# Half of the Strassen weight sums of the down projections: from VectorE to accumulating transfers

## What is computed

```python
def swiglu(h, w_gate, w_up, w_down):
    return (jax.nn.silu(h @ w_gate) * (h @ w_up)) @ w_down   # h: 256 x 2048, w_down: 5632 x 2048

h = rmsnorm(x, norm_ffn_pre[l])
x = x + rmsnorm(swiglu(h, w_ffn_gate[l], w_ffn_up[l], w_ffn_down[l]), norm_ffn_post[l])
```

## Time and profile before

| | |
|---|---|
| time, median of 3 runs | 2452.81 us (2452.26 to 2452.99) |
| time of the profiled execution | 2453.34 us |
| its span in the trace | 2451.5 us |
| TensorE busy | 2408.9 us (98%) |
| VectorE busy | 1799.5 us (73%) |
| ScalarE busy | 1223.0 us (50%) |
| GpSimd busy | 99.2 us (4%) |
| read from HBM | 503.06 MB |

### The profile page before, as it was taken

How to read it: one execution, slowest core, us unless ns; L and a number is a source line. 1 busy time by engine, 2 the same in 40 slices (tenths; PEclk the granted TensorE clock), 3 DMA queues, 4 the chain that set the end, 5 groups by cost and what they waited for, 6 DMA issues and landing times.

```text
span 2451.5 us, 28699 instructions
## 1 busy us (share of the span) xinstructions
PE 2408.9 (98%) x11138; PEld 1998.8 (82%) x11138; DVE 1799.5 (73%) x2366; ACT 1223.0 (50%) x1587; POOL 99.2 (4%) x150
## 2 busy tenths in 40 slices
PE   5999999999999999999999999999999999999998
PEld 4888888888788888888888888888888888888887
DVE  6998988766776675767777678965776766758776
ACT  4757665445544444444444544544544444445443
POOL 1210000000000000000000212000000000000000
PEclk8999999999999999999999999999999999999999
DMA  9997655564565566555656655445555565565654
GB/s 383 357 384 248 244 190 171 183 251 150 175 198 194 189 193 199 191 189 182 231 187 208 197 189 193 168 148 196 182 196 189 192 198 194 189 195 182 223 189 155
DMA packets 189495, 507.06 MB, mean 207 GB/s; under 512 B 17792, under 2 KB 18080, under 8 KB 188080
## 3 DMA queue, kind: packets, MB, share of 16 engines
q1 hardware_dynamic: 177008, 456.92, 55.3%
q0 software_dynamic: 11824, 46.14, 5.1%
q10 hardware_dynamic: 528, 2.16, 0.2%
HBM read 503.06 MB, written 2.10 MB: 206 GB/s over the span
## 4 chain that ended last, share of the span: by engine, by line
PE 95%; DVE 3%; DMA 1%; ACT 0%; issue 0%; SPq 0%; DVEq 0%; ACTq 0%
PE acc L677 29%; PE acc L679 29%; PE acc L678 29%; PE wk L1119 1%; PE wk L1118 1%; PE wk L1120 1%; DVE gate L1798 1%; PE wk L703 1%; DMA raw<-in_ada_w 1%; DMA raw<-in_w_in 1%; PE acc L1119 1%; PE acc L1118 1%; PE acc L1120 1%; DVE lo L1823 0%; PE wk L1190 0%
## 5 line engine op out<-in xcount | busy, mean ns | idle before, releaser
L677 PE MATMUL acc<-hi,h 128*128 128x512 f32 x2592 | 1017.3, 392 | 2.1 <-ACT proj L1384 0.7
L679 PE MATMUL acc<-hi,h 128*128 128x512 f32 x2592 | 1009.6, 389 | 0.0
L678 PE MATMUL acc<-lo,h 128*128 128x512 f32 x2592 | 1009.0, 389 | 0.0
L1823 DVE SCALAR_TENSOR_TENSOR lo<-raw,gcols,hi 128x1024 fp32r<-128x1024 f32 (+1 forms) x464 | 569.1, 1270 | 184.1 <-ACT hi L1269 181.5
L1269 ACT ACTIVATE hi<-raw,gcols 128x1024 fp32r<-128x1024 f32 (+1 forms) x464 | 497.4, 1128 | 380.7 <-PE acc L679 315.5
L1821 DVE TENSOR_TENSOR lo<-raw,hi 128x1024 fp32r<-128x1024 f32 (+2 forms) x428 | 486.7, 1187 | 121.8 <-ACT hi L1269 120.2
L677 PEld LDWEIGHTS acc<-hi,h 128*128 128x128 f32 x2592 | 486.9, 188 | 104.6 <-issue 3.7
L679 PEld LDWEIGHTS acc<-hi,h 128*128 128x128 f32 x2592 | 486.6, 188 | 102.2
L678 PEld LDWEIGHTS acc<-lo,h 128*128 128x128 f32 x2592 | 486.9, 188 | 99.1
L1269 ACT ACTIVATE hi<-raw 128x1024 fp32r<-128x1024 f32 (+2 forms) x428 | 413.5, 1026 | 275.1 <-DMA raw<-in_w_ffn_down 114.8
L677 PE MATMUL acc<-hi,g_hi 128*128 128x512 f32 x544 | 211.9, 390 | 0.0
(11 more groups left out here) (369 smaller groups left out, 1589.6 us busy)
## 6 DMA issues: line engine op xcount, KB each, us to landing
raw<-in_w_ffn_gate SPq DMA_DIRECT2D x176, 512.0 KB, 3.8
raw<-in_w_ffn_up SPq DMA_DIRECT2D x176, 512.0 KB, 4.6
raw<-in_w_ffn_down SPq DMA_DIRECT2D x176, 512.0 KB, 5.0
raw<-in_w_in SPq DMA_DIRECT2D x144, 512.0 KB, 4.8
raw<-in_w_kv SPq DMA_DIRECT2D x64, 512.0 KB, 4.8
ada_raw<-in_ada_w POOLq DMA_DIRECT2D x38, 512.0 KB, 7.7
gate_raw<-in_ada_w POOLq DMA_DIRECT2D x32, 512.0 KB, 6.3
raw<-in_w_out SPq DMA_DIRECT2D x32, 512.0 KB, 5.1
```

The lines of the kernel that those rows point to most:

```text
L677: pe.matmul(o, l_hi, w_hi[:, c], start=first, stop=False, skip_group_check=loaded)
L678: pe.matmul(o, l_hi, w_lo[:, c], start=False, stop=False, skip_group_check=loaded)
L679: mm = pe.matmul(o, l_lo, w_hi[:, c], start=False, stop=last, skip_group_check=loaded)
L1823: ins = vec.scalar_tensor_tensor(out=lo[:, r, c], in0=raw[:, r, c], scalar=gcols[:, st.gain, k:k + 1], in1=hi[:, m % HI_SLOTS, c], op0=ALU ...
```

## The change

Two of the four sums are no longer made by VectorE. b12 + b22 is made by a transfer that reads b22 from HBM and adds it to b12 where that lies in SBUF. t1 is made in two steps: SyncE loads b11 from HBM into the place of t1, and a second accumulating transfer adds b12 to it. VectorE still makes t2 and t4.

- SyncE has one more transfer of 256 KB for every slab of sums, on the semaphore `sum_loaded`, issued when the place in the ring is free.
- GpSimd issues two accumulating transfers of 256 KB for each Strassen slab (`sums_by_transfer`), the first when the slab has landed, the second when b11 has landed too. Both count on `sums_landed`. It runs for group 0 ahead of the load of `gain_a` and for group 1 behind it.
- ScalarE waits for both transfers ahead of the high part of a Strassen slab; before, it waited for lines 1858 and 1859. VectorE waits for both ahead of t2.
- Some semaphores are merged (`post0_in` and `post1_in`, `r_d_last` and `r_d_mid`, `k2_rotated` and `q2_rotated`), with waits at the same points of the same engines.

```diff
@@ sync, for each slab m
             if is_sums(m):
+                sp.wait_ge(slab_used, m - RING + 1)
+                src, (a, b), how = slabs[m - 1][0].src(slabs[m - 1][1], slabs[m - 1][2], 0)
+                sp.dma_start(raw[:, place(m) % RING, 0:HALF], src[:, 0:HALF]).then_inc(sum_loaded, 16)
                 continue
@@ scalar, conv
             if is_sums(m):
-                act.wait_ge(sums_made, 2 * sum(is_sums(i) for i in range(m + 1)))
+                act.wait_ge(sums_made, sum(is_sums(i) for i in range(m + 1)))
...
             if sevens(m) is not None:
-                act.wait_ge(sums_made, 2 * sum(is_sums(i) for i in range(m)) + 1)
+                act.wait_ge(sums_landed, 32 * (sum(is_sums(i) for i in range(m)) + 1))
@@ vector, conv
             if sevens(m) is not None:
-                vec.wait_ge(sums_made, 2 * sum(is_sums(i) for i in range(m)) + 2)
+                vec.wait_ge(sums_made, sum(is_sums(i) for i in range(m)) + 1)
@@ vector, weight_sums
             vec.wait_ge(raw_landed[r], LANDED[m])
-            vec.wait_ge(slab_used, m + 1 - RING + 1)
-            step(vec.tensor_tensor(t1, b11, b12, ALU.add))
-            vec.tensor_tensor(b12, b12, b22, ALU.add).then_inc(sums_made, 1)
+            vec.wait_ge(sums_landed, 32 * (sum(is_sums(i) for i in range(m)) + 1))
             step(vec.tensor_tensor(t2, t1, b22, ALU.add))
             vec.tensor_tensor(t4, t2, b21, ALU.add).then_inc(sums_made, 1)
@@ gpsimd
+        def sums_by_transfer(l, g):
+
+            for s in SEVEN[g]:
+                m = number[st_down[l].name, g, s]
+                i = sum(is_sums(j) for j in range(m))
+                r, r1 = place(m) % RING, place(m + 1) % RING
+                if i:
+                    pool.wait_ge(sums_made, i)
+                top, bottom = (st_down[l].src(g, s, part)[0] for part in range(2))
+                pool.wait_ge(raw_landed[r], LANDED[m])
+                pool.dma_start(raw[:, r, HALF:GW], bottom[:, HALF:GW], accum_op=ALU.add).then_inc(sums_landed, 16)
+                pool.wait_ge(sum_loaded, 16 * (i + 1))
+                pool.dma_start(raw[:, r1, 0:HALF], top[:, HALF:GW], accum_op=ALU.add).then_inc(sums_landed, 16)
+
+        sums_by_transfer(0, 0)
         pool.wait_ge(slab_used, number["down0", 0, MIX_DONE + 2] + 1)
-        pool.dma_start(gain_a[:], t_in["norm_ffn_post_2"][0:1, :].to_broadcast([P, D])).then_inc(post0_in, 16)
+        pool.dma_start(gain_a[:], t_in["norm_ffn_post_2"][0:1, :].to_broadcast([P, D])).then_inc(post_in, 16)
+        sums_by_transfer(0, 1)
```

More of the change, by code:

```diff
@@ L416, in build @@
     m_gained = sem("m_gained")
-    gate_b_in, pool_in, post0_in, diff_in, post1_in = (
-        sem(n) for n in ("gate_b_in", "pool_in", "post0_in", "diff_in", "post1_in"))
+    gate_b_in, pool_in, post_in, diff_in = (
+        sem(n) for n in ("gate_b_in", "pool_in", "post_in", "diff_in"))
     vec_step, pool_step = sem("vec_step"), sem("pool_step")
@@ L440, in build @@
         sem(n) for n in ("sums_made", "side_made", "side_hi_made", "acc_paused"))
+    sum_loaded, sums_landed = sem("sum_loaded"), sem("sums_landed")
     stored = sem("stored")
@@ L450, in build @@
         sem(n) for n in ("r_turned", "r_act", "r_forget", "r_log"))
-    r_d_last, r_d_mid, r_exp, r_kl_ready = sem("r_d_last"), sem("r_d_mid"), sem("r_exp"), sem("r_kl_ready")
+    r_diffs, r_exp, r_kl_ready = sem("r_diffs"), sem("r_exp"), sem("r_kl_ready")
     r_ke_ready, r_qe_ready = sem("r_ke_ready"), sem("r_qe_ready")
@@ L457, in build @@
     r_at_clear, r_qb_ready = sem("r_at_clear"), sem("r_qb_ready")
-    k2_rotated, q2_rotated = sem("k2_rotated"), sem("q2_rotated")
+    rotated = sem("rotated")
     d_blocks = sem("d_blocks")
@@ L1529, in _ @@
             if m == T_RF + 9:
-                act.wait_ge(r_d_last, 1)
+                act.wait_ge(r_diffs, 1)
                 act.activation(r_kl[:], r_kl[:], ACT.Exp).then_inc(r_exp, 1)
             if m == T_RF + 10:
-                act.wait_ge(r_d_mid, 1)
+                act.wait_ge(r_diffs, 2)
                 act.activation(r_b[:], r_b[:], ACT.Exp).then_inc(r_exp, 1)
@@ L2274, in _ @@
                 vec.tensor_tensor(by_chunk(r_kl), b_c[:, :, CHUNK - 1:CHUNK].to_broadcast([P, chunks, CHUNK]), b_c,
-                                  ALU.subtract).then_inc(r_d_last, 1)
+                                  ALU.subtract).then_inc(r_diffs, 1)
             if m == T_RF + 9:
                 vec.tensor_tensor(by_chunk(r_e), b_c, b_c[:, :, CHUNK // 2 - 1:CHUNK // 2].to_broadcast([P, chunks, CHUNK]),
-                                  ALU.subtract).then_inc(r_d_mid, 1)
+                                  ALU.subtract).then_inc(r_diffs, 1)
             if m == T_RF + 10:
@@ L2434, in evac @@
                 vec.wait_ge(m_squares, 8 * norm_no + 4 * g + 2 * t + n + 1)
-                vec.wait_ge(gain_in, 16)
+                vec.wait_ge(*gain_in)
                 vec.tensor_tensor(buf[:, t, c], acc[:, b, :], gain[:, c], ALU.mult).then_inc(acc_free[b], 1)
@@ L2509, in ffn @@
                 post(g)
-            return m_evac(st_down[l], m_a, gain_a, (post0_in, post1_in)[l], 1 + 2 * l)
+            return m_evac(st_down[l], m_a, gain_a, (post_in, 16 * (l + 1)), 1 + 2 * l)
         skewed_turn(ffn(0), m_a, 1, 4, st_k)
@@ L2575, in k2_blocks @@
             if f == 0:
-                vec.wait_ge(k2_rotated, g + 1)
+                vec.wait_ge(rotated, g + 1)
             d_turn_blocks(lambda toks: kv[toks, g], k2T, g, f)
@@ L2581, in q2_blocks @@
             if f == 0:
-                vec.wait_ge(q2_rotated, g + 1)
+                vec.wait_ge(rotated, 2 + g + 1)
             d_turn_blocks(lambda toks: q2[toks, :, g * GW:(g + 1) * GW], q2T, g, f)
@@ L2636, in _ @@
         split(5, 4, 8)
-        skewed_turn(m_evac(st_o, m_g, gain_g, mix1_in, 2), m_g, 2, 6, st_gu[1])
+        skewed_turn(m_evac(st_o, m_g, gain_g, (mix1_in, 16), 2), m_g, 2, 6, st_gu[1])
         evac = ffn(1)
@@ L2721, in _ @@
         pool.wait_ge(diff_in, 16 * 7)
-        for buf, rotated, st in ((kv, k2_rotated, st_k), (q2, q2_rotated, st_q)):
+        for buf, st in ((kv, st_k), (q2, st_q)):
             for g in range(2):
@@ L2739, in _ @@
         pool.dma_start(gain_g[:], t_in["norm_mix_post_2"][1:2, :].to_broadcast([P, D])).then_inc(mix1_in, 16)
+        sums_by_transfer(1, 0)
         pool.wait_ge(slab_used, number["down1", 0, MIX_DONE + 2] + 1)
-        pool.dma_start(gain_a[:], t_in["norm_ffn_post_2"][1:2, :].to_broadcast([P, D])).then_inc(post1_in, 16)
+        pool.dma_start(gain_a[:], t_in["norm_ffn_post_2"][1:2, :].to_broadcast([P, D])).then_inc(post_in, 16)
+        sums_by_transfer(1, 1)
     block.__exit__(None, None, None)
```

## The result

The changed kernel takes 2509.97 us (median of 4 runs, 2508.70 to 2511.73) against 2452.9 before: ratio 1.0234, 95% interval 1.0216 to 1.0251. It is 57 us slower. I had said 2464 and a range up to 2483. The direction was right, the size was five times too small.

The account below looks back on a forecast made before the run. TensorE, busy throughout the down projections, was taken to bound the kernel, so only late slabs could cost time: 4.5 (mixing) + 8 x 0.88 (waits) = 11.5 us, giving 2464 us; own range 2458 to 2483, with the hidden case 2451 to 2483.

Parts of the forecast that it names:

- The removed sums: Two VectorE sums for each of 20 Strassen slabs, 27 us in all, beside TensorE's work: worth 0.
- The margin of a Strassen slab: Down projections, kernel before: low part ready at 1288.09, TensorE comes to the slab at 1292.88, margin 4.8 us.
- the bound of 6.12 us on L: Down projections: TensorE waits for a Strassen slab once L is above 9.93 - 3.81 = 6.12 us.
- L: Time from the landing of a Strassen slab to the landing of both its accumulating transfers.
- The mixing: VectorE's copy and line 1898 sums, needed in slab 17; late L adds at most 4.5 us over both projections.
- L = 7.0: Forecast from 0.05 + 0.53 us and a second landing of 6.4 us, giving e = 0.88.
- the two rows that I had weighed: Trace landings of 512 KB GpSimd pairs: 4.9 us without a SyncE load just before, 7.3 with one.
- So waits alternate: e, 0, e, 0: Strassen slabs, e = L - 6.12: a wait gives the next slab 15.64 + e, just in time; four groups cost 8e.
- b11 lands before or with GpSimd's first issue: SyncE's 20 b11 loads, issued 12 matmuls (2.7 us) after the slab's own load, cost nothing.
- my sum: Added time 4.5 us for the mixing plus 8e for waits in the four groups; forecast 11.5 us.
- Slow accumulation: Rival: accumulating transfers run well under half a copy's rate; adds 43.5 us or rather more, 2496; chance 0.14.
- Its L of 11: Slow-accumulation rival's L, from the row of 1 MB loads and 1.4 us more.

Follow-up runs that it names:

- the kernel with fewer bytes: Changed kernel with both accumulating transfers cut to 128 of 512 columns, the sums of the other columns left out: 2466.41 us, ratio 1.0054.
- The kernels with added matmuls: Zero-weight matmuls ahead of the changed kernel's 16 later Strassen slabs, nine 2504.23 us, five 2504.93; nine with transfers for s = 6 and 12 alone, 2483.79.

## Why the prediction was right or wrong

**Right.** The removed sums were worth nothing: VectorE is not on the path, and TensorE has no wait that they could shorten. The margin of a Strassen slab and the bound of 6.12 us on L: where every second slab is transferred, L of about 9.1 gives waits of 3.0 us, and in the kernel with fewer bytes L of 6.6 to 7.7 gives 0 to 1.3. The mixing is the small item (1.4 us measured, at most 4.5 said).

**"L = 7.0" was mis-sized.** It measured 8.8 to 9.4 where the two transfers are issued one behind the other. Each term was a little larger than put: GpSimd starts 0.5 us after the landing (0.05 put), an accumulating issue takes 0.87 (0.53), the second landing is 7.3 to 8.2 (6.4; of the eight in the kernel with every second slab one took 6.7). Of the two rows that I had weighed, that of the busy copies, 7.3, was the right one. That an accumulating transfer costs more than a copy of its size is shown; whether by its second read or by the addition, no run separates. The Trainium skill's rule on reducing transfers ("Collectives: The Full Stack", section "The bandwidth ceiling: the fold count and why AG ≠ RS ≠ AR") gives about half the rate for a reducing ring transfer and pointed to that row. Issued right behind the first transfer, the plain copies of the same size landed in 5.8 us in the mean and the accumulating ones in 7.8: a third more and not the double. With L = 9.1 my sum gives 4.5 + 8 x 3.0 = 28.5 us, half of the measured 57.

**"So waits alternate: e, 0, e, 0" failed, and with it "b11 lands before or with GpSimd's first issue".** The slab is asked for before TensorE's wait, b11 after it. If TensorE waits a time x for a Strassen slab, the next slab's own load is on its way, but the place of t1 comes free x later, and so b11 comes x later. The gap between the two issues was 0.5 to 6.7 us and not 0.53. The time that a wait gives back to the one path it takes from the other. That path is 12 matmuls + b11 + transfer + 3.9 us, 18.94 in the chain shown, for 15.64; the mean from one Strassen slab to the next over the 16 is 15.64 + 3.24. Taking b11 out (with one of the additions) left 28 of 57 us; where only every second slab is transferred, so that no wait stands right before, the waits are of one length, which L alone explains; and in group 1 of the kernel in which ScalarE copies b11, both additions kept, the waits alternate as forecast.

**The clock was missing.** The sum has no term for it. Behind eight of the nine waits of 2.2 us and more TensorE went on at 1.2 GHz, behind none of the shorter ones (up to 2.0), which costs 14.7 us directly. The length of the wait alone does not tell: in the other kernels' traces one of 1.9 us (b11 by ScalarE) was followed by half clock and one of 3.3 (every second slab) was not. The half clock also lengthens the path through b11, whose first 12 matmuls then take 4.6 us in place of 2.7, and so the next wait.

**The rivals.** "Slow accumulation" comes nearest by its time (2496 and more), but not by its mechanism: issued right behind the first, the second transfer landed in 7.3 to 8.2 and not in 10.4 us. Its L of 11 is the measured mean by coincidence, since 2 us of that are the wait for b11. No rival had the second path.

What stays open: how the half clock and the path through b11 share the rest. The kernels with added matmuls remove the first by adding work, so that what they gain is a lower bound; and no kernel kept both additions in both groups while freeing the place of t1 early.

## What to carry to other kernels

Work taken from an engine that is not on the path is worth nothing, while the latency put in its place is paid as soon as it exceeds the slab's margin, 6.1 us here, which two small transfers in a row used up at 9. When a wait is reckoned to give time back later, check each input of the next step: one that is asked for only after the wait gives nothing back, and one such input can turn a wait now and then into one at every step. And a wait of TensorE costs more than its length when the clock falls behind it.

## What the runs showed of the hardware

- A 256 KB transfer from GpSimd landed in 3.2 us at best as a copy and 4.1 as an accumulation, and mostly took 5 to 8 beside other loads; 64 KB accumulated took 4.6 and 5.5 (medians) beside the same loads and 2.6 at best. A quarter of the bytes saved about 2 us of a landing of 8.
- An accumulating issue kept GpSimd 0.87 us (1.2 right behind another), a plain one 0.54. GpSimd's issue began 0.5 us after the landing that it waited for.
- Adding 16 us of matmuls that do nothing, where TensorE would stand idle, made a kernel 11 us faster in the median.
